# Expert choice from sorted logits, GpSimd making the gather's low half, and bias traffic moved to GpSimd's queue in a one-core encoder trunk

## What is computed

```python
bias = jnp.transpose(rel_bias_table[t5_bucket(rel)], (2, 0, 1))     # used in every attention
...
def moe_swiglu(h, router_w, w_gate, w_up, w_down):
    logits = (h @ router_w).astype(f32)
    top_val, top_idx = lax.top_k(logits, TOP_K)                     # 2 of 8
    top_w = jax.nn.softmax(top_val, axis=-1)
    gates = jnp.sum(jax.nn.one_hot(top_idx, N_EXPERTS, dtype=f32) * top_w[..., None], axis=-2)
    for e in range(N_EXPERTS):
        y = y + gates[..., e:e + 1].astype(h.dtype) * swiglu(h, w_gate[e], w_up[e], w_down[e])
...
x * lax.rsqrt(jnp.mean(x * x, axis=-1, keepdims=True) + EPS) * ln_final
```

## Time and profile before

| what | value |
|---|---|
| median of 3 runs | 1173.56 us |
| the profiled execution: time | 1173.32 us |
| its span, first to last instruction | 1171.5 us |
| TensorE matmul busy | 1152.5 us (98%) |
| VectorE / ScalarE / GpSimd busy | 957.4 / 828.5 / 44.6 us |
| memory read / written | 348.35 / 9.31 MB |

### The profile page before, as it was taken

One profiled execution on the slowest core, in us unless ns is written; L12 is line 12 of the kernel. 1 busy time (PEld: TensorE's weight loads), 2 busy tenths in 40 slices (PEclk: granted clock), 3 DMA queues, 4 the chain that ended last, 5 costly groups with the idle time before them and its releaser, 6 DMA issues.

```text
span 1171.5 us, 18160 instructions
## 1 busy us (share of the span) xinstructions
PE 1152.5 (98%) x5954; PEld 969.0 (83%) x5954; DVE 957.4 (82%) x1066; ACT 828.5 (71%) x1003; POOL 44.6 (4%) x61
## 2 busy tenths in 40 slices
PE   8999999999999999999999999999999999999996
PEld 7997888888998688888888888888888888888785
DVE  5867555544676899999899989989999989998996
ACT  6655544443654788888788888878888878888785
POOL 0400000000030000000000000000000000000000
PEclk9999999999999999999999999999999999999999
DMA  9965677555444299999999999999999999999960
GB/s 283 371 194 165 196 249 274 186 186 187 158 161 145 93 364 371 392 373 370 345 368 370 364 400 371 352 354 357 378 395 366 371 339 377 371 367 393 381 268 37
DMA packets 144295, 352.79 MB, mean 301 GB/s; under 512 B 6766, under 2 KB 65342, under 8 KB 144144
## 3 DMA queue, kind: packets, MB, share of 16 engines
q1 hardware_dynamic: 141808, 341.81, 80.8%
q0 software_dynamic: 2032, 9.23, 2.2%
q10 hardware_dynamic: 368, 0.62, 0.1%
HBM read 348.35 MB, written 9.31 MB: 305 GB/s over the span
## 4 chain that ended last, share of the span: by engine, by line
PE 92%; DVE 2%; DMA 2%; ACT 2%; issue 1%; DVEq 0%; SPq 0%; ACTq 0%; POOLq 0%
PE psum L1252 89%; PE psum L1249 3%; DMA scratch<-oe,row_e 1%; DMA raw<-in_w_in 1%; DMA back<-scratch 1%; DVE w_lo L430 0%; ACT w_hi L403 0%; DVE proj L1033 0%; ACT L740 0%; DVE w_lo L412 0%; ACT proj L740 0%; ACT aT_hi L726 0%; DVE x_sb L926 0%; ACT o_sq L734 0%; DVE proj L1040 0%
## 5 line engine op out<-in xcount | busy, mean ns | idle before, releaser
L430 DVE TENSOR_TENSOR w_lo<-raw,w_hi 128x1024 fp32r<-128x1024 f32 x528 | 630.8, 1221 | 45.3 <-PE psum L1252 13.8
L423 ACT ACTIVATE w_hi<-raw 128x1024 fp32r<-128x1024 f32 x528 | 550.3, 1061 | 100.3 <-PE psum L1252 99.2
L1252 PE MATMUL psum<-w_hi,aT_hi 128*128 128x512 f32 (+1 forms) x1232 | 445.6, 371 | 4.0 <-ACT w_hi L403 1.7
L1252 PE MATMUL psum<-w_hi,aT_lo 128*128 128x512 f32 (+1 forms) x1232 | 438.6, 365 | 0.0
L1252 PE MATMUL psum<-w_lo,aT_hi 128*128 128x512 f32 (+1 forms) x1232 | 322.2, 365 | 1.6 <-DVE w_lo L430 1.6
L1252 PEld LDWEIGHTS psum<-w_hi,aT_hi 128*128 128x128 f32 x1232 | 232.3, 189 | 41.6 <-issue 3.5
L1252 PEld LDWEIGHTS psum<-w_hi,aT_lo 128*128 128x128 f32 x1232 | 232.5, 189 | 35.1
L1252 PEld LDWEIGHTS psum<-w_lo,aT_hi 128*128 128x128 f32 x1232 | 214.0, 189 | 40.5 <-DVE w_lo L430 3.1
L412 DVE TENSOR_TENSOR w_lo<-raw,w_hi 128x1024 fp32r<-128x1024 f32 x118 | 144.9, 1234 | 47.7 <-PE psum L1252 45.9
L403 ACT ACTIVATE w_hi<-raw 128x1024 fp32r<-128x1024 f32 x118 | 124.5, 1059 | 81.4 <-PE psum L1252 74.2
L1252 PE MATMUL psum<-w_hi,heT_hi 128*128 128x512 f32 x352 | 137.8, 391 | 0.0
(11 more groups left out here) (194 smaller groups left out, 618.9 us busy)
## 6 DMA issues: line engine op xcount, KB each, us to landing
raw<-in_exp_w_down SPq DMA_DIRECT2D x88, 1024.0 KB, 7.3
raw<-in_exp_w_gate SPq DMA_DIRECT2D x80, 1024.0 KB, 6.7
raw<-in_exp_w_up SPq DMA_DIRECT2D x80, 1024.0 KB, 7.3
raw<-in_w_in SPq DMA_DIRECT2D x17, 1024.0 KB, 5.4
raw<-in_ffn_w_gate SPq DMA_DIRECT2D x22, 512.0 KB, 4.1
raw<-in_ffn_w_up SPq DMA_DIRECT2D x22, 512.0 KB, 5.1
raw<-in_ffn_w_down SPq DMA_DIRECT2D x11, 1024.0 KB, 5.0
raw<-in_w_out SPq DMA_DIRECT2D x8, 1024.0 KB, 12.0
```

The lines of the kernel that those rows point to most:

```text
L423: nc.scalar.activation(w_hi[:, q % HIGHS, :], raw_piece(slot, q % 2), ACT.Copy).then_inc(hi_made, 1)
L430: eng.tensor_tensor(w_lo[:, q % LOWS, :], raw_piece(e_slot[q // 2], q % 2), w_hi[:, q % HIGHS, :].bitcast(F32), ALU.subtract).then_inc(lo_ ...
L1252: return pe.matmul(dst, a, b, start=start, stop=stop, skip_group_check=True)
```

## The change

The bias table and the bias write and read-back go from SyncE's queue to GpSimd's (ahead of the router's weights); `ln_mix` goes to ScalarE's queue. SyncE no longer waits in the head. The choice uses an instruction that sorts eight values (`max`): once on the logits, once on keys made from the comparison with the second value, the rank order and 16 for the largest. `hot1` and `hot2` are made behind `mask`. GpSimd makes `xg_lo`, each tile as soon as its `xg_hi` is there, ahead of its routing work. `gather` multiplies all high parts, then the low parts by output tile. The end's variance takes one linked step less after the last squares, the correction one of five less.

```diff
@@ block.sync
             load_x(0)
-            sp.dma_start(gain_rows[0:2 * DK, :], ln_mix...).then_inc(g_landed, 16)
             load_x(1)
-            sp.dma_start(table_sb[:], rel_bias_table).then_inc(t_landed, 16)
             for u, (kind, layer, v) in enumerate(front):
                 slot = u % RING
-                if u == 4:
-                    sp.wait_ge(rows_out, 2)
-                    sp.dma_start(skew..., bias_rows[:]).then_inc(skew_written, 16)
                 if u == 5:
-                    sp.wait_ge(skew_written, 16)
...
-                    for h in range(2):
...
-                        sp.dma_start(bias[64 * h:64 * h + 64, :, :], src).then_inc(bias_landed, 16)
                     sp.dma_start(cst[:, P:C_ALL], consts[:, P:C_ALL]).then_inc(c_landed, 16)
@@ block.gpsimd
+            pool.dma_start(table_sb[:], rel_bias_table).then_inc(table_landed, 16)
             pool.dma_start(sink_all[:], ...).then_inc(sinks_landed, 16)
...
+            pool.wait_ge(rows_out, 2)
+            pool.dma_start(skew..., bias_rows[:]).then_inc(skew_written, 16)
+            pool.wait_ge(skew_written, 16)
+            for h in range(2):
...
+                pool.dma_start(bias[64 * h:64 * h + 64, :, :], src).then_inc(bias_landed, 16)
...
             pool.dma_start(gain_last, ln_final.partition_broadcast(P)).then_inc(gain_landed, 16)
+            for t in range(TT):
+                pool.wait_ge(xg_hi_made, t + 1)
+                pool.tensor_tensor(xg_lo[:, t, :], xg[:, t, :], xg_hi[:, t, :].bitcast(F32), ALU.subtract).then_inc(xg_lo_made, 1)
             pool.wait_ge(mask_made, 1)
...
+            pool.wait_ge(hots_made, 2)
             pool.tensor_tensor(row_parts[:, 0, :, :], mask, row, ALU.mult).then_inc(row_links, 1)
@@ block.scalar
+            act.dma_start(gain_rows[0:2 * DK, :], ln_mix...).then_inc(g_landed, 16)
@@ block.vector
-            def first_largest(values, top, hot):
...
-            first_largest(lg, top1, hot1)
-            link(dve.scalar_tensor_tensor(out=rest, in0=hot1, scalar=-3e38, in1=lg, op0=ALU.mult, op1=ALU.add))
-            first_largest(rest, top2, hot2)
-            dve.tensor_tensor(mask, hot1, hot2, ALU.add).then_inc(mask_made, 1)
-            link.also(dve.tensor_tensor(diff, top2, top1, ALU.subtract))
+            ranked_keys, ties, keys = rt[2][:], rt[3][:], rt[4][:]
...
+            for t in range(TT):
+                both(t, dve.max(ranked_keys[:, t, :], lg[:, t, :]))
+            link.also(dve.tensor_tensor(diff, rest[:, :, 1], rest[:, :, 0], ALU.subtract))
+            for t in range(TT):
+                link.also(dve.scalar_tensor_tensor(out=keys[:, t, :], in0=lg[:, t, :], scalar=rest[:, t, 1:2], in1=order[:, t, :],
+                                                   op0=ALU.is_ge, op1=ALU.mult))
+            for t in range(TT):
+                both(t, dve.tensor_scalar(ties[:, t, :], lg[:, t, :], rest[:, t, 0:1], 16.0, ALU.is_equal, ALU.mult))
+            link(dve.tensor_tensor(keys, keys, ties, ALU.add))
+            for t in range(TT):
+                both(t, dve.max(ranked_keys[:, t, :], keys[:, t, :]))
+            dve.tensor_tensor(mask, keys, wide(rest[:, :, 1]), ALU.is_ge).then_inc(mask_made, 1)
+            dve.tensor_tensor(hot2, keys, wide(rest[:, :, 1]), ALU.is_equal).then_inc(hots_made, 1)
+            dve.tensor_tensor(hot1, keys, wide(rest[:, :, 0]), ALU.is_equal).then_inc(hots_made, 1)
             norm_factor(3)
...
-            for t in range(TT):
-                dve.wait_ge(xg_made, t + 1)
-                dve.wait_ge(xg_hi_made, t + 1)
-                dve.tensor_tensor(xg_lo[:, t, :], xg[:, t, :], xg_hi[:, t, :].bitcast(F32), ALU.subtract).then_inc(xg_lo_made, 1)
...
+            dve.wait_ge(squared, 4 * TT + 2)
+            link(dve.tensor_scalar(ssum[:], ssum_end[:, 0, :], 1.0 / D_MODEL, EPS, ALU.mult, ALU.add))
             dve.wait_ge(squared, 4 * TT + 4)
-            link(dve.tensor_tensor(ssum[:], ssum_end[:, 0, :], ssum_end[:, 1, :], ALU.add))
-            dve.tensor_scalar(rstd[:, 0, :], ssum[:], 1.0 / D_MODEL, EPS, ALU.mult, ALU.add).then_inc(var_made, 1)
+            dve.scalar_tensor_tensor(out=var, in0=ssum_end[:, 1, :], scalar=1.0 / D_MODEL, in1=ssum[:],
+                                     op0=ALU.mult, op1=ALU.add).then_inc(var_made, 1)
             dve.wait_ge(root_made, 5)
-            factor(rstd[:, 0, :], rstd[:, 1, :], newton[:, 0, 0:2], rstd[:, 2, :]).then_inc(rstd_made, 1)
+            link(dve.reciprocal(fac, rstd[:, 1, :]))
+            link(dve.scalar_tensor_tensor(out=scratch, in0=fac, scalar=-0.5, in1=fac, op0=ALU.mult, op1=ALU.mult))
+            link(dve.tensor_tensor(scratch, scratch, var, ALU.mult))
+            dve.scalar_tensor_tensor(out=fac, in0=scratch, scalar=1.5, in1=fac, op0=ALU.add, op1=ALU.mult).then_inc(rstd_made, 1)
@@ block.tensor, gather
-                for part, t in ((0, 0), (0, 1), (1, 0), (1, 1)):
...
+                for t in range(TT):
                     for k in range(DK):
                         dst = psum[:, k // 2, (k % 2) * SEQ:(k % 2 + 1) * SEQ]
+                        mm(dst, xg_hi[:, t, k * P:(k + 1) * P], pick[:, t, :], t == k % 2 == 0, False)
+                pe.wait_ge(xg_lo_made, TT)
+                for k in range(DK):
+                    for t in range(TT):
+                        dst = psum[:, k // 2, (k % 2) * SEQ:(k % 2 + 1) * SEQ]
+                        ins = mm(dst, xg_lo[:, t, k * P:(k + 1) * P], pick[:, t, :], False, t == k % 2 == 1)
+                    if k % 2 == 1:
+                        ins.then_inc(gathered, 1)
```

More of the change, by code:

```diff
@@ L318, in trunk @@
         gain_landed, rw_landed = sem("gain_landed"), sem("rw_landed")
+        table_landed = sem("table_landed")
         sinks_landed, product_out = sem("sinks_landed"), sem("product_out")
@@ L558, in rope @@
                     pool.wait_ge(roped, done)
+            pool.wait_ge(rows_out, 2)
+            pool.dma_start(skew.rearrange("(p h) q r -> (h q) p r", h=2), bias_rows[:]).then_inc(skew_written, 16)
+            pool.wait_ge(skew_written, 16)
+            flat = skew.rearrange("(p h) q r -> h p (q r)", h=2)
+            for h in range(2):
+                src = flat[h, :, 63:63 + 64 * (REL - 1)].rearrange("p (q r) -> q p r", r=REL - 1)[:, :, 0:128]
+                pool.dma_start(bias[64 * h:64 * h + 64, :, :], src).then_inc(bias_landed, 16)
             first = 0
@@ L929, in _ @@
             dve.memset(aT_lo[:, DK - 2:DK, :].bitcast(F32), 0.0).then_inc(zeros_made, 1)
-            dve.wait_ge(t_landed, 32)
+            dve.wait_ge(t_landed, 16)
+            dve.wait_ge(table_landed, 16)
             dve.tensor_copy(table_rows[:], table_sb[:].unsqueeze(2).to_broadcast([N_BUCKETS, ATT_HEADS, 64])).then_inc(rows_ready, 1)
@@ L1097, in wide, with both @@
                 return c.unsqueeze(2).to_broadcast([P, TT, N_EXPERTS])
-            def first_largest(values, top, hot):
-                link(dve.tensor_reduce(top, values, AX, ALU.max))
-                for t in range(TT):
[L1102 to L1106, removed]
-            first_largest(lg, top1, hot1)
-            link(dve.scalar_tensor_tensor(out=rest, in0=hot1, scalar=-3e38, in1=lg, op0=ALU.mult, op1=ALU.add))
-            first_largest(rest, top2, hot2)
-            dve.tensor_tensor(mask, hot1, hot2, ALU.add).then_inc(mask_made, 1)
-            link.also(dve.tensor_tensor(diff, top2, top1, ALU.subtract))
+            ranked_keys, ties, keys = rt[2][:], rt[3][:], rt[4][:]
+            def both(t, ins):
+                if t == TT - 1:
+                    link(ins)
+                else:
+                    link.also(ins)
+            for t in range(TT):
[12 more added lines that the diff above has]
+            dve.tensor_tensor(hot1, keys, wide(rest[:, :, 0]), ALU.is_equal).then_inc(hots_made, 1)
             norm_factor(3)
@@ L1165, in _ @@
             dve.tensor_copy(passes_i[:], passes_f[:]).then_inc(route_ready, 1)
-            for t in range(TT):
-                dve.wait_ge(xg_made, t + 1)
-                dve.wait_ge(xg_hi_made, t + 1)
-                dve.tensor_tensor(xg_lo[:, t, :], xg[:, t, :], xg_hi[:, t, :].bitcast(F32), ALU.subtract).then_inc(xg_lo_made, 1)
             link.also(dve.tensor_scalar(posx[:, :, 8:16], posx[:, :, 0:8], -float(P), None, ALU.add))
             dve.wait_ge(e2_made, 1)
+            dve.wait_ge(hots_made, 2)
             link(dve.tensor_scalar(total, e2, 1.0, None, ALU.add))
@@ L1516, in gather @@
                 pe.wait_ge(picked, count)
-                for part, t in ((0, 0), (0, 1), (1, 0), (1, 1)):
-                    if part == 1:
-                        pe.wait_ge(xg_lo_made, t + 1)
+                for t in range(TT):
                     for k in range(DK):
                         dst = psum[:, k // 2, (k % 2) * SEQ:(k % 2 + 1) * SEQ]
-                        tokens = (xg_lo if part else xg_hi)[:, t, k * P:(k + 1) * P]
-                        first_one, last_one = part == t == k % 2 == 0, part == t == k % 2 == 1
```

(5 more changed lines are left out.)

7 lines of the change are left out of this document (3 added, 4 removed).

## The result

The changed kernel takes 1177.25 us (median of 7 runs, 1174.95 to 1177.92), the kernel before beside it 1173.14 us (7 runs, 1172.63 to 1174.26). The ratio is 1.0027, with a 95% interval of 1.0016 to 1.0039: slower, by about 0.3%, and above the predicted range, which ended at 1176.0. Against the profiled execution of before (1173.32, span 1171.5) it lost 1.9 us.

The account below looks back on a forecast made before the run. TensorE, carrying 92% of the chain, was taken as the bound, so only its idle time counts. 1173.32 - 1.87 (head) + 2.6 (routing) - 0.39 (end) = 1173.66, stated as 1173.7; range 1169.8 to 1176.0.

Parts of the forecast that it names:

- Head, -1.87: Start of the kernel: earlier first weights and unit 5 save 1.87 us, bounds 0 and 1.94.
- The 1.07: Head: TensorE's wait for the transposes, behind ScalarE's late unit 5, goes; 1.07 us saved, bounds 0 and 1.07.
- the 0.8: Head: first weight load starts 0.97 earlier behind two fewer small loads; 0.8 us saved, bounds 0 and 0.87.
- my reason for the lower bound: Head, first weights: gain 0 if the DMA engines' rate and not the issue set the landing.
- the 34.5 allowed: Head: bias through GpSimd's queue is there by 34.5 at the latest, before VectorE needs it; cost nothing.
- Choice, -0.3: Routing, VectorE's choice without contention: 2.0 against 2.42 us, net gain 0.3 at the gather.
- The port, +3.2 at the mask: Routing: VectorE's `diff` and sum of keys wait for GpSimd's two xg_lo instructions; mask 3.2 us later; exclusion's chance 0.56.
- Gather, -0.7: Gather to first expert: first pair complete sooner, VectorE freed of xg_lo; 0.7 us saved, bounds 0.4 and 0.95.
- The clock: Routing rival: TensorE stands 3.3 us, its clock falls, ranking to gather slow by 2.5 to 6, taken 3.5; chance 0.09.
- the rival that I had priced at 1177.2: TensorE's clock falls after standing 3.3 us before the ranking; 3.5 us slower, time 1177.2; chance 0.09.
- Experts, 0: Stretch of the experts: the forecast's sum has no term for it.
- End, -0.39: Behind the last matmul: two linked steps of 0.20 go, 0.39 us saved, bounds 0.3 and 0.45.

Follow-up runs that it names:

- the cut-up version: Changed kernel with GpSimd's two xg_lo instructions each cut into four of 256 columns; 1176.08 us against 1173.38 for the kernel before.
- the keys in PSUM: Changed kernel with the choice's keys kept in PSUM and the difference of top values moved behind the mask; 1175.53 us against 1173.59 for the kernel before.
- The run without idle matmuls: Kernel before with the ten idle matmuls behind the turned logits taken away; 1174.90 us against 1173.21, ratio 1.0014.
- the one with 26: Changed kernel with 26 idle matmuls in place of 10 behind the turned logits; 1174.90 us against 1173.38 for the kernel before.
- the fill: Kernel before with three idle float32 matmuls behind the second half's transposes in the head; 1173.73 us against 1173.59.
- the choice's kernel: Kernel before with only the choice's part (two sorts in place of twice first_largest), xg_lo on VectorE; 1172.69 us against 1173.21, ratio 0.9999.

## Why the prediction was wrong, step by step

*Head, -1.87.* Measured -1.63 at the end of the transposes (34.19 against 35.82) and -1.73 before the routing. The 1.07 went whole, though ScalarE's wait for unit 5, which I had expected to go, shrank only from 4.42 to 3.37. The first piece gave 0.40 of the 0.8: the load was issued 0.96 sooner but took 7.58 to land instead of 7.01, so the rate, my reason for the lower bound, took about half of it. All this holds for a head at full clock; a fall there cost 1.3 to 2.0 us in the traces above, and the prediction had no term for it. The bias did land in time: its write took 7.8 us in place of 4.1 on the other queue and the reads 6.2, at about 33.5, inside the 34.5 allowed and before VectorE's score at 37.82.

*Choice, -0.3.* Alone it gave 0.39 at the gather.

*The port, +3.2 at the mask.* Measured +2.89, by the mechanism and at the two instructions named: `diff` until the end of GpSimd's first, the sum until the end of its second. GpSimd needed 2.3 to 2.4 us for a tile (2.35 forecast). I had put the pairs of keys and ties at 0.74; they took 0.61, and the sorts 0.25 for two in place of 0.4. The kernel before with xg_lo on GpSimd shows that it is not the sort; the cut-up version and the keys in PSUM show that it is the pair of inputs and the hold of a single instruction.

*Gather, -0.7.* At full clock it is -0.92 (4.82 against 5.74), within my bounds. ScalarE was ready in time. Alone it gives nothing, since it needs VectorE freed of xg_lo; so in these runs this gain and the port's loss come from the same move, and no version was found that has the one without the other.

*The clock, left out of the sum.* This is the step that failed. I gave the fall 0.09 and argued from one row, where 4.6 us had passed behind the last matmul, and from the lack of a fall in one trace of a kernel whose idle times in the routing were filled. The idle time I worked out (3.3 us; 3.02 measured) lay between two points, and I took it for safe. The run without idle matmuls shows a fall behind 2.60 us of standing, without any port; the one with 26 shows that the port's wait, with the clock held in the routing, ends at 1174.90, inside the range. The fall costs the changed kernel 1.42 us in the gather of its profiled execution and, by the run with 26 against the kernels before beside each, 2.6 us of median.

So the rival that I had priced at 1177.2 is what happened, together with the forecast's own port wait. That its number is so near the 1177.25 measured is in part luck. I took 3.5 us for the clock, and the trace has 1.42. What the median has beyond this trace, 2.05 us, is not located. The kept traces show two candidates: a longer stretch at 1.2 GHz, 6.8 us in the kernel before with xg_lo on GpSimd and in the cut-up version against 3.4 here, and a second fall in the head, 1.70 us with 26 idle matmuls.

*Experts, 0.* +0.67 in the profiled execution. The waits of TensorE list it: two waits for `w_lo` with 2.3 us in total, the longest 2.0, against 1.6 and 1.3 before. They stand where VectorE waits for the first rows read back from memory: write and read took 8.24 and 7.40 us there against 8.06 and 6.89. The other traces settle that this is no work of the change: the same stretch took 758.06 us before and 758.73 after, and 757.58 to 759.26 in the eleven other traces without a fall of the clock in it. The kernel before with only the head, the gather's order or the fill altered has 758.56, 758.69 and 758.67. What makes the stretch vary was not looked into.

*End, -0.39.* Measured -0.43.

With a clock that holds, the sum of what was measured is 1173.32 - 1.73 + 2.93 - 0.92 - 0.43 = 1173.2, half a microsecond from the forecast of 1173.7. It is a sum over traces and no run. The nearest run, with 26 idle matmuls, has a profiled execution of 1174.90; less the 1.70 that the fall in the head cost it, that is the same 1173.2.

## What to carry to other kernels

Work that is moved from VectorE to GpSimd isn't free where VectorE runs a chain of small instructions at that time: each one with two inputs from SBUF waits for the whole of GpSimd's instruction. Price it by pairing the two timelines, and look for a stretch without such a chain. Putting an operand in PSUM, or cutting GpSimd's instruction up, is not enough when more such instructions follow: both runs only moved the wait behind the mask. A new wait ahead of TensorE is also a question to the clock: fill it, or count the slower matmuls behind it as part of the price. One trace without a fall doesn't show that an idle time is safe, since other executions of the same code can fall.

The best version tried is the changed kernel with xg_lo left on VectorE, 1171.70 us against 1173.38 for the kernel before; with the fill in the head it was as good (1171.98 against 1173.59).

## What the runs showed of the hardware that was not expected

- The granted clock fell where TensorE had stood 2.02 us (at the transposes, at 35.6), 2.60 (no idle matmuls) and 3.02 (changed kernel). The length of the gap alone doesn't tell: in the head, with a wait of 1.69 us for the first piece, it fell at 11.4 in the choice's kernel and not in the kernel before, whose trace has the same 1.69.
- Nor does the gap tell which matmuls pay. In the changed kernel the clock fell 2.1 us after TensorE had work again, without idle matmuls 0.9 after; with xg_lo on GpSimd alone it fell 2.1 us into the gap, and the first matmuls behind it were the slow ones.
- VectorE's scalings with one SBUF input wait too when they run from SBUF to SBUF beside GpSimd: L901 took 0.66 in the cut-up version, and the first scaling of the end (L1244 of the changed kernel) 0.68, until GpSimd's two instructions there ended, against 0.17. It ended ahead of the last squares, so it cost nothing. RECIPROCAL, one input too, passed in 0.15 beside GpSimd in the cut-up version. The Trainium skill, "SBUF — State Buffer", section "Who interferes with whom", counts `tensor_scalar` among the operations that can take the port pair shared with GpSimd. The trace agrees, 0.66 and 0.68 in place of 0.17.
- A wait lasted to the end of a GpSimd instruction of 2.3 to 2.4 us: 2.21 us for a VectorE instruction of 0.16. By the same section of the Trainium skill, "SBUF — State Buffer", whoever begins first has the pair for the whole of its instruction. The run agrees, well beyond what the trace of before could show.
- The same 384 KB write landed in 7.8 us from GpSimd's queue, with the weight loads running beside it, against 4.1 from SyncE's, which had held the loads back until then. No run parts the queue from the loads.
